# The arena's base rounded up to a multiple of 128 bytes

## What is computed

```python
# first block
h = layer_norm(ALPHA * x + 0.5 * swiglu(x, ffn1_w_gate, ffn1_w_up, ffn1_w_down))   # 2816 hidden
proj = h @ w_in                                  # 1024 x 3072: queries, forget gates, values, gates, u, v
mix = concat([hgrn2(...), spatial_gating(...)]) @ w_out
h = layer_norm(ALPHA * h + mix)
m = layer_norm(mem)                              # 256 memory rows
xa = softmax((h @ wq) @ (m @ wk).T / 16) @ (m @ wv) @ wo     # 4 heads of 256
h = layer_norm(ALPHA * h + xa)
h = layer_norm(ALPHA * h + 0.5 * swiglu(h, ffn2_w_gate, ffn2_w_up, ffn2_w_down))
# second block
q, k, v, u = split(rmsnorm(h) @ w_in_2)          # 8 query heads of 64, 2 key/value heads, rope
x = h + concat([attention(q, k, v), pool_mixer(u)]) @ w_out_2
x = x + (silu(rmsnorm(x) @ w_gate) * (rmsnorm(x) @ w_up)) @ w_down
```

## Time and profile before

| | us |
|---|---|
| median of 3 runs | 1688.51 |
| lowest and highest | 1688.37, 1689.0 |
| span of the profiled execution | 1686.8 |
| TensorE with a matmul under way | 1668.9 |
| ScalarE, VectorE, GpSimd busy | 597.0, 644.4, 697.5 |

### The profile page before, as it was taken

One profiled execution on the slowest core, in us unless ns is written; L12 is line 12 of the kernel. 1 busy time (PEld: TensorE's weight loads), 2 busy tenths in 40 slices (PEclk: granted clock), 3 DMA queues, 4 the chain that ended last, 5 costly groups with the idle time before them and its releaser, 6 DMA issues.

```text
span 1686.8 us, 20746 instructions
## 1 busy us (share of the span) xinstructions
PE 1668.9 (99%) x8353; PEld 1397.9 (83%) x8353; DVE 644.4 (38%) x1067; ACT 597.0 (35%) x911; POOL 697.5 (41%) x385
## 2 busy tenths in 40 slices
PE   9999999999999999999999999999999999999998
PEld 7888888899888888899888888888768988888887
DVE  4111111267665776656111211276763512121122
ACT  4222222247445464436222122256573422122220
POOL 4453444446563353025443444433321544344432
PEclk9999999999999999999999999999999999999999
DMA  7333233333221454123333243332112333324322
GB/s 206 91 98 100 76 112 100 88 117 104 66 76 51 126 155 131 38 75 99 91 99 100 69 119 100 90 117 63 44 32 57 106 100 98 90 81 119 93 82 76
DMA packets 296521, 157.58 MB, mean 93 GB/s; under 512 B 5233, under 2 KB 293098, under 8 KB 296426
## 3 DMA queue, kind: packets, MB, share of 16 engines
q1 hardware_dynamic: 296426, 156.26, 32.0%
HBM read 154.14 MB, written 2.10 MB: 93 GB/s over the span
## 4 chain that ended last, share of the span: by engine, by line
PE 92%; ACT 3%; DVE 3%; issue 1%; POOL 0%; DMA 0%; SPq 0%; DVEq 0%; ACTq 0%
PE bank L480 22%; PE bank L481 22%; PE bank L484 22%; PE bank L2234 2%; PE bank L2231 2%; PE bank L2230 2%; PE bank L523 2%; PE bank L524 2%; PE bank L528 2%; PE bank L2673 2%; PE bank L509 1%; PE bank L503 1%; PE bank L504 1%; PE bank L2661 1%; PE bank L2421 1%
## 5 line engine op out<-in xcount | busy, mean ns | idle before, releaser
L410 POOL TENSOR_TENSOR wlo<-wraw,whi 128x1024 fp32r<-128x1024 f32 (+1 forms) x252 | 595.4, 2376 | 827.6 <-ACT whi L405 827.6
L480 PE MATMUL bank<-ahi,whi 128*128 128x512 f32 x1294 | 508.1, 393 | 0.0
L481 PE MATMUL bank<-alo,whi 128*128 128x512 f32 x1294 | 504.0, 389 | 0.0
L405 ACT CAST whi<-wraw 128x1024 fp32r<-128x1024 f32 (+1 forms) x284 | 284.6, 1026 | 240.3 <-PE bank L484 154.6
L484 PE MATMUL bank<-ahi,wlo 128*128 128x512 f32 x1294 | 321.1, 389 | 0.0
L480 PEld LDWEIGHTS bank<-ahi,whi 128*128 128x128 f32 x1294 | 243.0, 188 | 51.5 <-issue 1.4
L481 PEld LDWEIGHTS bank<-alo,whi 128*128 128x128 f32 x1294 | 243.0, 188 | 51.5 <-issue 1.4
L484 PEld LDWEIGHTS bank<-ahi,wlo 128*128 128x128 f32 x1294 | 242.9, 188 | 50.6
L1543 DVE SCALAR_TENSOR_TENSOR hval<-gate,bank 128x512 f32<-128x512 f32 x66 | 45.4, 687 | 553.0 <-PE bank L484 541.9
L959 ACT ACTIVATE gate<-bank 128x512 f32<-128x512 f32 x66 | 39.6, 600 | 507.6 <-PE bank L484 500.1
L1552 DVE SCALAR_TENSOR_TENSOR res<-res,bank 128x512 f32<-128x512 f32 x80 | 54.1, 686 | 254.6 <-PE bank L484 181.2
(11 more groups left out here) (341 smaller groups left out, 2201.1 us busy)
## 6 DMA issues: line engine op xcount, KB each, us to landing
wraw<-in_ffn_w_gate SPq DMA_DIRECT2D x43, 512.0 KB, 3.7
wraw<-in_ffn_w_up SPq DMA_DIRECT2D x43, 512.0 KB, 3.7
wraw<-in_w_in SPq DMA_DIRECT2D x34, 512.0 KB, 3.8
wraw<-in_ffn_w_down SPq DMA_DIRECT2D x32, 512.0 KB, 3.6
wraw<-in_w_gate SPq DMA_DIRECT2D x22, 512.0 KB, 3.7
wraw<-in_w_up SPq DMA_DIRECT2D x22, 512.0 KB, 3.8
wraw<-in_w_out SPq DMA_DIRECT2D x16, 512.0 KB, 4.0
wraw<-in_w_down SPq DMA_DIRECT2D x16, 512.0 KB, 3.6
```

The lines of the kernel that those rows point to most:

```text
L405: eng.copy(whi[:, b % 4, 0:n], wraw[:, b % RAW, 0:n]).then_inc(hi_ready, 1)
L410: eng.tensor_tensor(wlo[:, b % RAW, 0:n], wraw[:, b % RAW, 0:n], whi[:, b % 4, 0:n], ALU.subtract).then_inc(LO[b][0], 1)
L480: eng.matmul(o, w, xhi[:, k, :], start=(k == 0), stop=False)
L481: eng.matmul(o, w, xlo[:, k, :], start=False, stop=False)
```

## The change

The arena's base is rounded up to the next multiple of P = 128 bytes. All arena tiles move up by 64 bytes, from 113856 to 113920 for the base. Nothing else is changed.

```diff
@@ -125,7 +125,7 @@
         mst = sb("mst", [P, 4, 6])
         mmv = sb("mmv", [P, 2, 2])
         mrs = sb("mrs", [P, 2])
-        arena = top[0]
+        arena = -(-top[0] // P) * P
         ARENA = nc.sbuf_usable_end - arena

         def region(start):
```

## The result

The kernel became slower. The median over five runs each is 1694.89 us (1694.36 to 1696.8) after the change and 1688.37 us (1687.94 to 1689.0) before it, a ratio of 1.0039 with a 95% interval of 1.0027 to 1.0052. The profiled execution spans 1693.1 us, where it spanned 1686.8.

What follows compares the result with a forecast made beforehand. TensorE was taken to bound the kernel, its time a sum of matmul spacings. Gains of 4.57 us less losses of 0.50 and 1.06 us gave 1688.51 - 3.01 = 1685.5 us, own range 1684.7 to 1686.6, with rivals 1683.8 to 1688.9.

Steps and rivals of the forecast that it cites:

- What bounds the kernel: TensorE has work in 1668.9 of 1686.8 us and 92% of the chain; time is a sum of matmul spacings.
- The sorting into even and odd: Operand pairs with the same residue modulo 128 bytes are even, others odd; all become even and take even spacing.
- Hid, 512 columns: Down blocks moving hid against whi: 228.9 to 226.7 ns for 1392 matmuls, 2.99 us gained after step-in costs.
- The hand-overs: Where an up part follows a down part, six times: 50 ns saved each, 0.30 us gained.
- The output projection: It alternates between odd and even pairs; six blocks fall from 5.548 to 5.44 us, 0.64 us gained.
- The value stage: Memory value stage, stationary operand in the arena: 233.3 to 226.7 ns for 96 matmuls, 0.64 us gained.
- Hid, 256 columns: 384 matmuls moving hid lose 2.1 ns each, 0.80 us; 0.30 us is hidden by waits, 0.50 us lost.
- Mhi: Memory keys, 256 columns: 113.3 to 120.0 ns for 144 matmuls, plus the first pair; 1.06 us lost, on the chain.
- The other engines: VectorE, ScalarE and GpSimd: a residue is worth at most 1% of an instruction; put at 0, 0.1 us either way.
- Rival 1: Nothing moves: something else sets hid's spacing, or the period exceeds 128 bytes; 1688.5 us, chance 0.17.
- Rival 2: Slower: period 256 bytes, distance 128 worse than 64; hid at 512 columns adds 6.1 us, 1694.6 us, chance 0.08.
- Rival 3: The gains come and the 256-column losses don't: 4.57 us faster, 1683.9 us, chance 0.08.

Runs made afterwards that it cites:

- arena_192: Arena base 192 bytes above that of the kernel before, all operand pairs at distance 0 modulo 256; 1686.99 us, ratio 0.9989.
- arena_320: Arena base 320 bytes above that of the kernel before, 256 above that of the changed one; 1694.71 us, ratio 1.0034.
- hid_back: The changed kernel with hid alone moved back by 64 bytes, to distance 64 from whi; 1688.55 us, ratio to before 1.0001.
- weights_128: Kernel before with 128 unused bytes between alo and wraw; ahi and alo come to distance 128, hid keeps 64; 1709.35 us, ratio 1.0123.
- weights_64: Kernel before with 64 unused bytes between alo and wraw; ahi and alo come to distance 192, hid keeps 64; 1709.89 us, ratio 1.0125.
- arena_128: Arena base 128 bytes above that of the kernel before, distance 192 for hid and 64 for the value stage; 1692.79 us, ratio 1.0024.
- memory_192: Arena base 192 bytes above that of the kernel before, with mhi and mlo 192 bytes further on; 1685.88 us, ratio 0.9981.

## Why the prediction was wrong, step by step

- **What bounds the kernel** was right. A change of addresses with no instruction changed moved the time by 6.5 us, and all of it is TensorE's spacing. The clock took part only in a short stretch.
- **The sorting into even and odd** is where it failed. The rows were sorted by the residue modulo 128, and the step "I assume that a pair that becomes even takes the even spacing of its width" carried that over to a distance that no row had. The even pairs of before were all at distance 0, not at a multiple of 128. arena_192 at d = 0 has the forecast's spacings, the change at d = 128 does not. A warning lay in the rows: the earlier trace rows are both odd and show 228.9 and 233.3 ns. The forecast took them as two sizes of one class. They are one tile 64 bytes ahead and one 64 bytes behind, so the class was not what set the spacing. The period of 256 bytes and the sign would both have followed from asking why they differ.
- **Hid, 512 columns** (2.99 us gained) came out as 5.6 us lost, by this step. At d = 0 it is 2.0 + 1.0 = 3.0 us gained (228.95 to 226.92 and 229.25 to 226.73 ns).
- **The hand-overs** (0.30 us) stayed, 2.31 for 2.32 us, since hid is still not in step with ahi.
- **The output projection** (0.64 us) fell to 5.525 us a block for 5.548, some 0.14 us over six. shi and slo did not come to d = 0.
- **The value stage** (0.64 us gained) stayed at 2.80 us: from d = 192 to 128 there is next to no difference (233.3 ns in both; 232.3 in arena_320). In arena_192 it fell to 2.72.
- **Hid, 256 columns** (0.50 us lost): 0.3 us, at 118.6 in place of 120 ns. d = 128 has its own value here, too.
- **Mhi** (1.06 us lost): 1.0 us, and on the chain as forecast. But the number is luck: mhi came to d = 128 and not to 0, and that it ran at the 120.0 ns of d = 0 there was one of two values; in arena_320 and hid_back it is 118.7 at the same distance.
- **The other engines** (0) and the loads: right. The GpSimd line above is the largest of them.
- **Rival 1** (nothing moves, 0.17) had one right condition, a period longer than 128 bytes, but took from it that nothing would move, which the runs rule out. By the Trainium skill's page "SBUF — State Buffer", section "Who interferes with whom", the moving operand and the weight load have ports of their own and TensorE never waits on anyone. The runs do not agree: hid's spacing goes from 226.7 to 228.9 to 233.3 ns by the distance of these two operands alone.
- **Rival 2** (slower, 0.08) is what happened, by its own mechanism: the period is 256 bytes, and a distance of 128 is worse than 64. Its 4.4 ns were 4.1 and 3.8. Its 1694.6 us against 1694.9 is closer than its working deserves, since it left out mhi and the 256-column halves (+1.3 us) and the gain of ahi (-0.6 us). It was worked out from rows and had one argument against it, that all rows sort by 64 bytes; but no row could have told 128 from 256, as the text of rival 1 said. For a case that the rows could not exclude, 0.08 was too little, and with it the range would have reached 1694.6.
- **Rival 3** (gains without the 256-column losses, 0.08) is wrong at d = 0: in arena_192 hid and mhi go to 120.0 ns. That one distance can have two values with 256 columns, its argument, holds at 64, 128 and 192.

## What to carry to other kernels

Where TensorE is the bound, with fp32r matmuls that each load their weights as here, put the moving tile and the tile of its weights at starts that differ by a multiple of 256 bytes when 512 columns move; "rounded up to 128" can be worse than not rounded. Sort spacings by the signed distance itself rather than by a class that is thought to explain it, and when two members of a class differ, the class is wrong. When a gain on the bound engine doesn't arrive, look at the stops that it now reaches earlier, and at the granted clock right behind them.

## What the runs showed of the hardware

- The spacing of fp32r matmuls depends on the signed distance of the two operands modulo 256 bytes: with 512 columns 226.7 ns at 0, 228.9 at 64, and 232.3 to 234.3 elsewhere, about 3% more than at 0. For ahi's and alo's 4056 matmuls at 128 or 192 that was 21 us (weights_128, weights_64). What in the chip has this period was not tested, and no run shows it. Only hid was seen one whole period apart (64 and 320, 128 and 384).
- With 256 columns the order is another one: 0 gives 120 ns, as dear as any, and 192 gives 113.4 or 117.8 (arena_128, weights_64).
- With 256 columns and d = 64 a stage runs steadily at 113.3 or at 117.8 ns. Hid and mhi changed places between before and weights_64. What picks the one or the other stays open.
- A stop of 2.3 us ahead of the memory keys was followed by 3.4 us at the lower granted clock in the traces of arena_192 and memory_192, 1.57 us lost in the former. The stop of 2.1 us at the same place in before was not.
